# TensorE transpositions in plain float32 or in the rounded 32-bit type, in a two-layer streaming encoder step

## What is computed

```python
h = _rmsnorm(x, g_attn[l])
fq, fk, fv, flf, mq, mckv, mkpe, sq, sk, sv = _mixer_inputs(h, pos, ...)   # z = h @ w_in, D = 1024
o_a = _sweep(fq, fk, fv, True, jnp.cumsum(flf, axis=1))
o_b = _sweep(mq, *_mla_kv(mckv, mkpe, w_ukv[l]), False)
o_c = _swa_prompt(sq, sk, sv, rel_bias, swa_sinks[l])
x = x + _merge(o_a, o_b, o_c, w_out[l])
x = x + _mlp(_rmsnorm(x, g_mlp[l]), w_up[l], w_down[l])                    # relu squared, D_FF = 4096
```

## Time and profile before

| what | value |
|---|---|
| median of three runs | 2847.08 us |
| profiled execution, span | 2845.6 us |
| TensorE matmuls, busy | 2736.4 us (96%), 14966 instructions |
| TensorE weight loads, busy | 2210.4 us (78%) |
| VectorE, busy | 1745.5 us (61%) |
| ScalarE, busy | 1057.2 us (37%) |
| GpSimd, busy | 1047.5 us (37%) |
| granted TensorE clock, mean | 0.991 |

### The profile page before, as it was taken

How to read it: one execution, slowest core, us unless ns; L and a number is a source line. 1 busy time by engine, 2 the same in 40 slices (tenths; PEclk the granted TensorE clock), 3 DMA queues, 4 the chain that set the end, 5 groups by cost and what they waited for, 6 DMA issues and landing times.

```text
span 2845.6 us, 39618 instructions
## 1 busy us (share of the span) xinstructions
PE 2736.4 (96%) x14966; PEld 2210.4 (78%) x14966; DVE 1745.5 (61%) x2196; ACT 1057.2 (37%) x1968; POOL 1047.5 (37%) x594
## 2 busy tenths in 40 slices
PE   8998999999999999999999989999999999999997
PEld 6986666787888887888779766667878888878886
DVE  4036777634564559888740467765355564688887
ACT  4225544424323333333332255544243223333333
POOL 1111000114544456767511210001145444667666
PEclk9999999999999999999999999999999999999999
DMA  4212001432333456343132200014423433653441
GB/s 142 64 29 65 20 17 44 135 133 97 122 136 126 152 179 240 132 140 128 63 114 63 66 23 17 17 44 135 151 79 137 155 118 137 245 188 132 137 148 74
DMA packets 164722, 308.75 MB, mean 109 GB/s; under 512 B 24720, under 2 KB 90416, under 8 KB 164592
## 3 DMA queue, kind: packets, MB, share of 16 engines
q1 hardware_dynamic: 161280, 303.59, 31.0%
q10 hardware_dynamic: 3312, 3.41, 0.4%
HBM read 207.40 MB, written 97.72 MB: 107 GB/s over the span
## 4 chain that ended last, share of the span: by engine, by line
PE 85%; DVE 7%; issue 3%; ACT 2%; POOL 1%; DMA 1%; SPq 0%; DVEq 0%; ACTq 0%; POOLq 0%
PE ps L2553 7%; PE ps L2557 7%; PE ps L2555 7%; PE ps L2463 7%; PE ps L2464 7%; PE ps L2465 7%; PE ps L2224 6%; PE ps L2074 6%; PE ps L2072 5%; PE ps L2073 5%; PE ps L2254 4%; PE ps L2277 4%; PE ps L2339 2%; PE ps L2191 1%; PE ps L2408 1%
## 5 line engine op out<-in xcount | busy, mean ns | idle before, releaser
L2553 PE MATMUL ps<-wq_hi,sa_hi 128*128 128x512 f32 x896 | 350.1, 391 | 5.3 <-DVE x L2006 5.3
L2555 PE MATMUL ps<-wq_lo,sa_hi 128*128 128x512 f32 x896 | 349.9, 391 | 0.0
L2557 PE MATMUL ps<-wq_hi,sa_lo 128*128 128x512 f32 x896 | 349.8, 390 | 0.0
L2006 DVE TENSOR_TENSOR x<-ps,x 128x1024 f32<-128x1024 f32 x224 | 264.1, 1212 | 55.0 <-PE ps L2557 50.6
L1944 DVE TENSOR_TENSOR sa_lo<-ra,sa_hi 128x1024 fp32r<-128x1024 f32 x112 | 281.3, 2513 | 23.8 <-ACT sa_hi L1447 23.8
L1059 POOL TENSOR_TENSOR wq_lo<-wsum,wq_hi 128x1024 fp32r<-128x1024 f32 x64 | 157.4, 2460 | 291.0 <-ACT wq_hi L1427 291.0
L2072 PE MATMUL ps<-w_hi,hT_hi 128*128 128x512 f32 (+2 forms) x672 | 248.7, 370 | 0.0
L2074 PE MATMUL ps<-w_hi,hT_lo 128*128 128x512 f32 (+2 forms) x672 | 246.1, 366 | 0.0
L2073 PE MATMUL ps<-w_lo,hT_hi 128*128 128x512 f32 (+2 forms) x672 | 245.3, 365 | 0.0
L1936 DVE TENSOR_TENSOR cq<-ps,cq 128x1024 f32<-128x1024 f32 x48 | 58.6, 1222 | 286.3 <-ACT cq L1488 244.2
L1065 POOL TENSOR_TENSOR wq_lo<-bsum,wq_hi 128x1024 fp32r<-128x1024 f32 x64 | 171.5, 2690 | 114.5 <-ACT wq_hi L1438 114.5
(11 more groups left out here) (324 smaller groups left out, 6262.7 us busy)
## 6 DMA issues: line engine op xcount, KB each, us to landing
ra<-hidden_scratch SPq DMA_DIRECT2D x112, 512.0 KB, 3.3
hidden_scratch<-cq SPq DMA_DIRECT2D x94, 512.0 KB, 2.7
rq<-in_w_up_dram SPq DMA_DIRECT2D x64, 512.0 KB, 3.9
rq<-in_w_down_dram SPq DMA_DIRECT2D x64, 512.0 KB, 4.3
residual_scratch<-x SPq DMA_DIRECT2D x27, 512.0 KB, 3.1
x<-residual_scratch SPq DMA_DIRECT2D x27, 512.0 KB, 7.6
x<-in_x_prompt_dram SPq DMA_DIRECT2D x16, 512.0 KB, 7.2
w_raw<-in_w_in_dram SPq DMA_DIRECT2D x16, 512.0 KB, 4.2
```

The source lines that it names most:

```text
L2553: pe.matmul(out, ah[:, k, :], bh[:, k * 512:(k + 1) * 512], start=new and k == 0, stop=False, skip_group_check=True)
L2555: pe.matmul(out, ah[:, k, :], bl[:, k * 512:(k + 1) * 512], start=False, stop=False, skip_group_check=True)
L2557: last = pe.matmul(out, al[:, k, :], bh[:, k * 512:(k + 1) * 512], start=False, stop=final and k == 1, skip_group_check=True)
```

## The change

A second identity, `identR`, is made by ScalarE from `identF`, in the type float32r. For every tile that is turned, a second name over the same bytes is declared in float32r (`bits`). A helper `turned` issues the transposition with the float32r names of source and identity and with the output in PSUM seen as float32r. Every call of `pe.transpose` goes through it. The copies out of PSUM, the waits and the order of instructions are as they were.

```diff
@@ -242,6 +242,7 @@
         identF = keep("identF", [P, P])
+        identR = keep("identR", [P, P], F32R)
@@ -382,6 +383,25 @@
+        def bits(name, offset, shape):
+            return at(f"{name}_bits", offset, shape, F32R)
+
+        pbuf_b = [bits(f"pbuf{i}", RING + i * 4096 if i < 3 else NRM, [P, NPT * P]) for i in range(4)]
+        hbuf_b = [bits(f"hbuf{i}", Z + 18432 + i * 4096, [P, D]) for i in range(2)]
...
@@ -1147,6 +1170,7 @@
             nc.scalar.copy(identB[:], identF[:])
+            nc.scalar.copy(identR[:], identF[:])
             nc.scalar.copy(cmaskB[:], constA[:]).then_inc(pro.sem, 1)
@@ -2065,6 +2089,10 @@
+            def turned(out, src):
+
+                return pe.transpose(out.bitcast(F32R), src, identR[:])
+
@@ -2081,8 +2109,7 @@
                     for k in range(KC):
-                        last = pe.transpose(out[:, k * P:(k + 1) * P], src[:, k * P:(k + 1) * P],
-                                            identF[:])
+                        last = turned(out[:, k * P:(k + 1) * P], src[:, k * P:(k + 1) * P])
                     last.then_inc(done.sem, 1)
@@ -2251,8 +2276,7 @@
                             c0 = (g * len(tiles) + b - tiles[0]) * P
-                            last = pe.transpose(bank(4 + ch % 2)[:, i * P:(i + 1) * P], pbuf[n % 4][:, c0:c0 + P],
-                                                identF[:])
+                            last = turned(bank(4 + ch % 2)[:, i * P:(i + 1) * P], pbuf_b[n % 4][:, c0:c0 + P])
                         last.then_inc(pt_mm.sem, 1)
...
```

More of the change, by code:

```diff
@@ L384, in hybrid_step @@
         qbds = at("qbds", LATT + 9216, [P, STREAMS, SWA_H, NEW])
+        def bits(name, offset, shape):
+            return at(f"{name}_bits", offset, shape, F32R)
+        pbuf_b = [bits(f"pbuf{i}", RING + i * 4096 if i < 3 else NRM, [P, NPT * P]) for i in range(4)]
+        hbuf_b = [bits(f"hbuf{i}", Z + 18432 + i * 4096, [P, D]) for i in range(2)]
+        h2buf_b = [bits(f"h2buf{i}", Z + 16384 + i * 4096, [P, D]) for i in range(2)]
+        stg0_b = [bits(f"stg0_{i}", Z + 27648 + i * 2048, [P, 512]) for i in range(2)]
+        stg3_b = [bits(f"stg3_{i}", RING + 32768 + i * 2048, [P, 512]) for i in range(2)]
+        zc_b = bits("zc", NRM, [P, NT, 416])
+        zsb_b = bits("zsb", Z + 69632, [P, 512])
+        zsb_end_b = bits("zsb_end", Z + 14336, [P, 512])
+        qtok_b = bits("qtok", RING + 16384, [P, MLA_H, QK_M])
+        wukv_b = bits("wukv", RING + 20480, [P, MLA_H, 2, HD])
+        fk_b = bits("fk_c", HT, [P, STREAMS, 2, 256])
+        ckv_b = bits("ckv_c", HT + 49152, [P, STREAMS, 2, KVR])
+        kr_b = bits("kr_c", HT + 57344, [P, STREAMS, 2, ROPE])
+        sk_b = bits("sk_c", HT + 59392, [P, STREAMS, 128])
+        pbufS_b = [bits(f"pbufS{i}", RING + 8192 + i * 1536, [P, 384]) for i in range(3)]
         ps = ctx.enter_context(nc.psum_tensor("ps", [P, 8 * 512], F32))
@@ L600, in x_done, with stg_b @@
             return dn_ev.at(l * NS, ((12, 13, 15, 16)[t // 2] if t < NPT else 14) - DN_EV)
+        def stg_b(m):
+            return (stg0_b if m < NT else stg3_b)[m % 2]
         def stg_stores_before(m):
@@ L2108, in tp_h1 @@
                 def tp_h1(t):
-                    transposes(bank(2 * (t % 2), 2), hbuf[t % 2], h1, h1.at(l, t + 1), tp1, (lo1, lo1.at(l, t - 1)) if t >= 2 else None)
+                    transposes(bank(2 * (t % 2), 2), hbuf_b[t % 2], h1, h1.at(l, t + 1), tp1, (lo1, lo1.at(l, t - 1)) if t >= 2 else None)
                 def stg_transposes(m):
@@ L2116, in stg_transposes @@
                     for k in range(4 if m < NT else 3):
-                        last = pe.transpose(bank(6 + m % 2)[:, k * P:(k + 1) * P], stg(m)[:, k * P:(k + 1) * P],
-                                            identF[:])
+                        last = turned(bank(6 + m % 2)[:, k * P:(k + 1) * P], stg_b(m)[:, k * P:(k + 1) * P])
                     last.then_inc(stg_tp.sem, 1)
@@ L2149, in _ @@
                     for k in range(3):
-                        pe.transpose(bank(t % 2)[:, k * P:(k + 1) * P], zc[:, t, k * P:(k + 1) * P], identF[:])
-                    pe.transpose(bank(t % 2)[0:96, 384:512], zc[:, t, 320:416], identF[:]).then_inc(lat_tp.sem, 1)
+                        turned(bank(t % 2)[:, k * P:(k + 1) * P], zc_b[:, t, k * P:(k + 1) * P])
+                    turned(bank(t % 2)[0:96, 384:512], zc_b[:, t, 320:416]).then_inc(lat_tp.sem, 1)
                     if t < NPT:
@@ L2197, in scores @@
                         for hh in range(MLA_H):
-                            last = pe.transpose(S[0:QK_M, hh * P:(hh + 1) * P], qtok[:, hh, :], identF[:])
+                            last = turned(S[0:QK_M, hh * P:(hh + 1) * P], qtok_b[:, hh, :])
                         last.then_inc(sc_mm.sem, 1)
@@ L2232, in wuk_transposes @@
                     for h in range(MLA_H):
-                        last = pe.transpose(bank(0, 2)[:, h * P:(h + 1) * P],
-                                            wukv[:, h].rearrange("p e d -> p (e d)"), identF[:])
+                        last = turned(bank(0, 2)[:, h * P:(h + 1) * P], wukv_b[:, h].rearrange("p e d -> p (e d)"))
                     last.then_inc(wk_mm.sem, 1)
@@ L2309, in cache_transposes @@
                                     col = ((e * 2 + c) * 2 + b) * P
-                                    last = pe.transpose(kt[:, col:col + P],
-                                                        fk_c[:, 2 * p + e, b, c * P:(c + 1) * P], identF[:])
+                                    last = turned(kt[:, col:col + P], fk_b[:, 2 * p + e, b, c * P:(c + 1) * P])
                     elif kind == "swa":
                         for e in range(2):
-                            last = pe.transpose(kt[:, e * P:(e + 1) * P], sk_c[:, 2 * p + e, :], identF[:])
+                            last = turned(kt[:, e * P:(e + 1) * P], sk_b[:, 2 * p + e, :])
                     else:
                         for b in range(2):
-                            pe.transpose(kt[:, b * P:(b + 1) * P], ckv_c[:, p, b, :], identF[:])
-                            last = pe.transpose(kt[0:ROPE, 256 + b * P:256 + (b + 1) * P], kr_c[:, p, b, :],
-                                                identF[:])
+                            turned(kt[:, b * P:(b + 1) * P], ckv_b[:, p, b, :])
+                            last = turned(kt[0:ROPE, 256 + b * P:256 + (b + 1) * P], kr_b[:, p, b, :])
                     last.then_inc(skt_mm.sem, 1)
@@ L2382, in stream_transposes @@
                     for k in range(2 if ITEMS[i][0] == "swa" else 3):
-                        last = pe.transpose(bank(4 + i % 2)[:, k * P:(k + 1) * P], pbufS[i % 3][:, k * P:(k + 1) * P],
-                                            identF[:])
+                        last = turned(bank(4 + i % 2)[:, k * P:(k + 1) * P], pbufS_b[i % 3][:, k * P:(k + 1) * P])
                     last.then_inc(spt.sem, 1)
@@ L2436, in tp_h2 @@
                         pe.wait_ge(bf_ok.sem, bf_ok.at(l, t - 1))
-                    transposes(h2bank(t), h2buf[t % 2], h2, h2.at(l, t + 1), tp2, free)
+                    transposes(h2bank(t), h2buf_b[t % 2], h2, h2.at(l, t + 1), tp2, free)
                 for n in range(2 * NT):
@@ L2541, in up_turn @@
                     for i in range(4):
-                        last = pe.transpose(bank(7)[:, quarter(i)], (zsb_end if end else zsb)[:, quarter(i)], identF[:])
+                        last = turned(bank(7)[:, quarter(i)], (zsb_end_b if end else zsb_b)[:, quarter(i)])
                     last.then_inc(up_mm.sem, 1)
```

## The result

Four runs of the changed kernel took 2821.30, 2825.62, 2827.75 and 2836.11 us, a median of 2826.68, against 2846.11 for the kernel before on the same chip: a ratio of 0.9934, interval 0.9922 to 0.9946. It is faster by 19.4 us, half of what was forecast (38 to 39 us), and inside the range. The mean granted TensorE clocks of these runs, in the same order, were 0.990, 0.989, 0.988 and 0.982: the slower a run, the lower its clock. The kernel before, in the 54 of its runs whose clock is listed, ran at 0.989 to 0.993.

A forecast was written before the change was run, and what follows sets the result against it. TensorE, busy 2736.4 of 2845.6 us, was taken to bound the kernel. 1454 x 27 ns = 39.3 us saved; 2845.6 - 39.3 + 1.5 = 2807.8, forecast 2808 us, range 2778 to 2851 us.

The forecast's parts named there:

- unit price: On TensorE, a rounded transposition costs 82 ns instead of 109 from start to start; 1926 of them save 52.0 us gross.
- a mixture of two prices: 82 ns per transposition: 67 ns (only the stream counts) weighted two thirds, 112 ns (long load needed) one third.
- The shares: Part of the saving that arrives per stage, 40% to 90%; 39.3 us in all, 12.7 us not arriving.
- The chain: In attention, L2254's share of the chain of waits falls from 21.5% towards 17%.
- Every product that is no transposition keeps its distances: Sign on TensorE: the start-to-start distances of all other products stay unchanged; if they move, the prediction is wrong altogether.
- The clock: Sign: TensorE's granted clock stays at 0.99 to 1.00 in the profile's windows; otherwise the prediction is wrong altogether.
- By stage: Shares arriving: input projection 85%, attention 40% up to 320 us and 85% after, streams 60%, output projection and MLP 90%.
- The hidden load (1): Transposition loads stay hidden altogether: 67 ns each, 2786 us; at the floor of 50 ns, 2761 us; chance 27%.
- no change (3): Transpositions keep their present pace or the long load takes over at 112 ns: 2847 to 2851 us; chance 16%.
- slower (4): Rival 4: rounded transpositions' long loads, poorly overlapped, make them 120 ns each, 2863 to 2868 us; chance 10%.
- Rival 2: VectorE and ScalarE take over in attention, nothing credited there arrives: 17 us saved, 2830 us; chance 11%.
- likeliest range: Whole kernel's time in the likeliest case, with 75 to 90 ns a transposition: 2796 to 2820 us.

## Why the prediction came out half as large as forecast

- **The unit price** was right: 84 ns for 82, from the pack of loads, and 52.1 us gross for 52.0. That the gross agrees so closely is luck: a step inside a block gained 24 ns with a 128-column load and 40 with one of 96, and the first transposition of a block, taken with the product ahead of it, 45 to 50 in most blocks, which the forecast did not tell apart. The reason given for the price held in part: the load shows, and it is the transposition's short one (140 ns printed, every 0.086 us) that sets the pace, not a mixture of two prices. Where the load is narrower the pace rises: 69 to 70 ns with 96 columns, 62 to 64 with 32.
- **The shares** were right in their sum and wrong in their reason. 12.7 us were to go into waits, 12.5 did. But most was expected at VectorE's probabilities, and that wait grew by 3.2; the rest is spread, as over hbuf, 10.4 before:

```profile
PE ps L2094 <- DVE pbuf L1757: 25.2, 36, 2.5
PE ps L2094 <- DVE hbuf L1629: 12.2, 5, 4.2
```

- **The chain** moved as said: L2254's 21.5% from 320 to 520 us are 17.0% now.

```profile
by line: PE ps L2250 31.9%; PE ps L2301 20.1%; PE ps L2094 17.0%; PE ps L2217 6.6%; DVE pbuf L1757 5.1%; issue 3.7%; DVE ptb L1745 3.6%; DVE pbuf L1789 3.3%; SPq L661 1.8%; PE ps L2265 1.0%; ACT pbuf L1338 1.0%; DVE rinv L1754 0.8%; ACT qto
```

- **The step that failed** is "Every product that is no transposition keeps its distances", and with it the sum, which took the gross, less waits, for the result. The products behind the blocks took 12.6 us back: the span should have been 2806.3 and was 2819.4, 13.1 us more. The rows for it stood there. The prediction saw that a load might show at 128 columns, but asked it only of a transposition behind a transposition, not of the product behind the last one.
- **The clock** was to be 0.99 to 1.00 in these windows; one is at 0.98. Over whole executions it fell from between 0.989 and 0.993 to between 0.982 and 0.990. Between the profiled execution (2821.30 us) and the median lie another 5.4 us, and they go with the clock.
- **By stage**, from TensorE's own instructions, both layers, forecast and measured: input projection 7.8 and 3.7 us, attention 22.6 and 18.3, streams 3.9 and -0.2, output projection and MLP 5.0 and 4.6. Of the missing 12.9 us the first three lack a little over 4 each. The border before the streams is the forecast's, at 520 us, where the weight is turned; drawn at the first cached keys, 5 us later, it gives the attention 15.7 and the streams 2.4.
- **The rivals.** The hidden load (1), no change (3) and slower (4) are refuted by the pack of loads. Rival 2 came within 4 us of the measured time (2830), closer than the forecast, but by luck and not by its cause: the attention gave 18.3 of the 26 us, and the wait that it needed, over 25 us more, did not come. Against rival 4 the prediction said that no product of their width has a shorter load than transpositions; the mask product has one, 98 ns against 141.
- **A sum.** With 75 ns a transposition the forecast's own terms give 2797.7 us, not the 2796 at which its likeliest range starts.

## What to carry to other kernels

When a short instruction becomes shorter, look at what its length had been covering at the end of its run: count the blocks, not only the instructions, and price the first load behind each. Here the products behind 306 blocks took back a quarter of the gross gain (12.6 of 52.1 us). And compare two versions at the same granted clock before a difference of under 1% is given a cause.

## What the hardware showed unexpectedly

- A load of a transposition is printed 140 ns long and one of a product 190, while their starts, where loads set the pace, are 86 and 110 ns apart: the printed end of a load is not when the next can begin.
- A plain transposition behind a rounded one takes 135 ns, against 109 behind its like.
- In kernels that differ in nothing but the type of the transpositions, the mean granted clock was 0.989 to 0.993 with plain ones (54 runs) and 0.982 to 0.990 with rounded ones (10 runs), and one stretch of some 28 us at 1.2 GHz came in two of the fourteen profiles of all variants. Why is not shown.
